# Split-operand matmuls that walk their columns from the last to the first

## What is computed

```python
for i in range(DEPTH):                      # DEPTH = 2
    h = rms_norm(x, attn_norm[i])
    proj = jnp.einsum('bsd,de->bse', h, w_in[i])          # 1024 x 3072
    sb = stick_breaking_attention(...)                    # 8 heads of 64
    df = differential_attention(...)                      # 4 heads of 2 x 64, values 128
    x = x + jnp.einsum('bse,ed->bsd', jnp.concatenate([sb, df], axis=-1), w_out[i])
    h2 = rms_norm(x, ffn_norm[i])
    if i % 2 == 0:
        x = x + swiglu(h2, dense_w_gate[j], dense_w_up[j], dense_w_down[j])    # width 2816
    else:
        x = x + moe_swiglu(h2, router_w[j], expert_w_gate[j], expert_w_up[j],
                           expert_w_down[j])              # top 2 of 8 experts, width 3584
return rms_norm(x, final_norm)
```

## Time and profile before

| | |
|---|---|
| median of the runs | 1404.23 us |
| span of the profiled execution | 1401.0 us |
| median less that span | 3.2 us |
| instructions in the trace | 19232 |

### The profile page before, as it was taken

The page is one execution under the profiler, slowest core; times in us unless marked ns, Lnnn a source line. Parts: engine busy times, 40 slices in busy tenths (PEclk is TensorE's granted clock), DMA queues, the critical chain, the costliest instruction groups (busy, mean ns, idle before and its releaser), DMA issues.

```text
span 1401.0 us, 19232 instructions
## 1 busy us (share of the span) xinstructions
PE 1386.3 (99%) x7369; PEld 1180.9 (84%) x7369; DVE 1139.5 (81%) x862; ACT 934.6 (67%) x751; POOL 37.4 (3%) x53
## 2 busy tenths in 40 slices
PE   9999999999999999999999999999999999999997
PEld 8888999889888888888888888888888888888885
DVE  6866565556857999888988888898888889889897
ACT  5555443445555877777777777777777777777775
POOL 0010000000010020000000000000000000001100
PEclk9999999999999999999999999999999999999999
DMA  9734985556424999999999999999999999999992
GB/s 336 265 114 147 393 326 187 191 170 199 155 98 163 356 389 393 396 394 397 371 395 390 361 387 392 374 371 389 394 350 396 391 361 383 393 378 364 396 395 114
DMA packets 191039, 448.80 MB, mean 320 GB/s; under 512 B 8515, under 2 KB 11274, under 8 KB 190986
## 3 DMA queue, kind: packets, MB, share of 16 engines
q1 hardware_dynamic: 189162, 441.74, 85.9%
q0 software_dynamic: 1616, 5.77, 1.0%
q10 hardware_dynamic: 208, 0.54, 0.1%
HBM read 429.67 MB, written 18.36 MB: 320 GB/s over the span
## 4 chain that ended last, share of the span: by engine, by line
PE 97%; DVE 1%; DMA 1%; ACT 1%; SPq 1%; issue 0%; DVEq 0%; ACTq 0%
PE ps L550 90%; PE ps L1009 2%; DMA raw<-in_w_in 1%; PE ps L681 1%; PE ps L712 0%; PE ps L968 0%; PE ps L735 0%; PE ps L670 0%; PE ps L639 0%; ACT w_hi L380 0%; PE ps L700 0%; PE ps L695 0%; PE ps L701 0%; PE ps L682 0%; PE ps L623 0%; PE ps L724 0%
## 5 line engine op out<-in xcount | busy, mean ns | idle before, releaser
L385 DVE TENSOR_TENSOR w_lo<-raw,w_hi 128x2048 fp32r<-128x2048 f32 x401 | 915.0, 2291 | 187.2 <-ACT w_hi L380 186.4
L380 ACT ACTIVATE w_hi<-raw 128x2048 fp32r<-128x2048 f32 x400 | 766.5, 1918 | 295.7 <-PE ps L550 286.7
L550 PE MATMUL ps<-w_hi,xe_hi 128*128 128x512 f32 x896 | 244.7, 395 | 0.6 <-DVE xe_lo L1846 0.6
L550 PE MATMUL ps<-w_hi,xe_lo 128*128 128x512 f32 x896 | 240.0, 390 | 0.0
L550 PE MATMUL ps<-w_lo,xe_hi 128*128 128x512 f32 x896 | 239.9, 389 | 0.0
L550 PEld LDWEIGHTS ps<-w_hi,xe_lo 128*128 128x128 f32 x896 | 168.2, 188 | 35.8
L550 PEld LDWEIGHTS ps<-w_lo,xe_hi 128*128 128x128 f32 x896 | 168.2, 188 | 35.4
L550 PEld LDWEIGHTS ps<-w_hi,xe_hi 128*128 128x128 f32 x896 | 164.6, 188 | 32.4 <-issue 0.8
L550 PE MATMUL ps<-w_hi,he_hi 128*128 128x512 f32 x448 | 120.9, 391 | 0.0
L550 PE MATMUL ps<-w_lo,he_hi 128*128 128x512 f32 x448 | 120.3, 390 | 0.0
L550 PE MATMUL ps<-w_hi,he_lo 128*128 128x512 f32 x448 | 120.1, 389 | 0.0
(11 more groups left out here) (250 smaller groups left out, 960.9 us busy)
## 6 DMA issues: line engine op xcount, KB each, us to landing
raw<-in_expert_w_gate SPq DMA_DIRECT2D x112, 1024.0 KB, 7.4
raw<-in_expert_w_up SPq DMA_DIRECT2D x112, 1024.0 KB, 7.5
raw<-in_expert_w_down SPq DMA_DIRECT2D x112, 1024.0 KB, 7.4
raw<-in_w_in SPq DMA_DIRECT2D x23, 1024.0 KB, 6.2
raw<-in_dense_w_gate SPq DMA_DIRECT2D x11, 1024.0 KB, 7.1
raw<-in_dense_w_up SPq DMA_DIRECT2D x11, 1024.0 KB, 7.6
raw<-in_dense_w_down SPq DMA_DIRECT2D x11, 1024.0 KB, 5.0
raw<-in_w_out SPq DMA_DIRECT2D x8, 1024.0 KB, 5.7
```

Source lines behind the costliest of these rows:

```text
L380: nc.scalar.activation(half_of(w_hi, n), raw[:, n % RAW, :], ACT.Copy).then_inc(hi_ready, 1)
L385: nc.vector.tensor_tensor(half_of(w_lo, n), raw[:, n % RAW, :], half_of(w_hi, n).bitcast(F32), ALU.subtract).then_inc(lo_ready, 1)
L550: return pe.matmul(o, stationary, moving, start=start, stop=stop, skip_group_check=True)
```

## The change

`add` now reverses the column axis of both the output and the moving operand. Column j of the product still lands at column j, but the engine takes the columns in falling order of address. The stationary operand and all other matmuls stay as they were. No instruction is added, removed or moved on any engine.

```diff
@@ -547,7 +547,7 @@
         def _(pe):
             def add(o, stationary, moving, start=False, stop=False):
 
-                return pe.matmul(o, stationary, moving, start=start, stop=stop, skip_group_check=True)
+                return pe.matmul(o[:, ::-1], stationary, moving[:, ::-1], start=start, stop=stop, skip_group_check=True)
 
             def keep_running(count, bank):
 
```

## The result

The changed kernel takes 1437.02 us (1436.02 to 1438.76, four runs) against 1404.56 us for the kernel before (1403.14 to 1405.26, four runs): a ratio of 1.0239, interval 1.0224 to 1.0253, or 32.5 us. The forecast was 1404 us in a range from 1340 to 1485, with 0.55 on no change.

A forecast was written before the change was run, and what follows sets the result against it. TensorE's matmuls were taken as the bound, L550 being 90% of the span. Terms 0 + 0 + 0 on the 1401.0 us span, plus 3.2 us up to the median of the runs, gave 1404 us, range 1340 to 1485.

The forecast's parts named there:

- Step (1), the reversed read: Reversed read and write in the 6504 matmuls of L550: no cost, 0.444 ns a column as now.
- The upper bound: Step (1) at the rate of L766's plain float32 products, 0.791 ns a column: L550 would take 990 us more.
- the gain: Case of a faster kernel, down to 1342 us; chance 0.15.
- the lost cycle: Rival with a slower kernel, 1479 us; chance 0.10, shared with smaller slowdowns at places not seen.
- The two arguments for zero: For step (1): backward jumps between matmuls are free, and the rate is the same for one bank or two in turn.
- f: Part of an L550 matmul's time that doesn't depend on its columns, from 113.4 and 227.1 ns: -0.3 ns, taken as nothing.
- Loss of pairing: Rival: falling moving reads or PSUM writes handle columns singly, not in pairs; 990 to 1270 us more, 2394 to 2674; chance 0.20.
- Steps (2) to (4): Between matmuls zero; VectorE and ScalarE as readers zero; any TensorE excess shows fully in the result.
- (2): Between matmuls: where turned follows unturned, order changes for one product only, delay at most 0.23 us; taken as zero.

The follow-up runs named there:

- e9: Kernel before plus 20 streams of 40 equal matmuls in front of the gather; 512 columns, 128 stationary: rising 227.5 ns, falling 233.5 ns per matmul.
- e13: Kernel before with moving and output columns in groups of 64, groups falling, rising inside: 1403.17 us against 1403.21, ratio 0.9999.
- e5: Kernel before with moving and output columns in groups of four (16 bytes), groups falling, rising inside: 1437.11 us.
- e7: Kernel before with moving and output columns in groups of sixteen (64 bytes), groups falling, rising inside: 1436.20 us.
- e2: Kernel before with only the output written in falling order, the moving operand read rising: 1403.25 us.
- e10: Kernel before with only the products that move 512 columns reversed, those of 256 columns left rising: 1435.50 us.
- e6: Kernel before with moving and output columns in groups of four (16 bytes), groups rising, falling inside: 1403.70 us.
- e12: Kernel before plus 19 streams of 40 matmuls, with shifted moving or stationary starts and groups of 64 falling; rising streams 9.09 to 9.46 us.
- e8: Changed kernel with the moved weight pieces placed 4 bytes further on in their slots: 1447.13 us.

## Why the prediction was wrong

- **Bound and path: right.** TensorE's column stream set the time, no new wait arose, the supply had slack, and the excess of the starts went straight into the result.
- **Step (1), the reversed read, is the step that failed.** I took its cost as nothing and forecast 1404 us. It is 6.3 ns for a product of 512 columns in the long stretches (27.4 us over all 4680) and up to 4.4 for one of 256 (6.2 us over all 1824). The upper bound held, but was too high by a factor of thirty (990 us against 33). That 1437 us lies within the range of 1340 to 1485 is luck. The two ends, the gain at 1342 us and the lost cycle at 1479, rest on a length of TensorE's clock cycle, and no run shows it. What the runs show in its place is the time of a column at 512 columns: 0.444 ns rising (227.1/512), 0.456 falling (233.4/512), 0.422 with bf16 in either direction (215.9/512, e9).
- **The two arguments for zero didn't bear on the question.** That the jump between products is free was read from f alone (next item). Falling groups of 256 bytes, with seven jumps backward in each 512-column product, do cost nothing (e13, 1403.17 us). That says nothing of the order within 256 bytes, where the price is (e5, e7). That the rate is the same for one PSUM bank and two was an argument on the write, which is free (e2, 1403.25 us).
- **f = -0.3 ns was a coincidence read as a law.** I took 113.4 and 227.1 ns as the nature of a product. The same chain had 117.8 ns for 144 rising products. A distance that comes in two sizes for one form asks for what makes it good, and thus for what could spoil it. The 0.444 ns a column that the pair gave was the falling price at 512 columns, 0.456 ns, less a discount.
- **The rivals.** Loss of pairing (0.20, 2394 us or more) is dead: even 16-byte pieces in falling order cost 3% (e5), not 80%. The lost cycle (0.10, 1479 us) was nearest in kind, a small additional price of a column, but it had 75 us where the two medians are 32.5 apart. The gain (0.15, down to 1342 us) isn't seen in any run: the lowest median of a kernel with turned reads is 1403.17 us (e13), beside 1403.21 for the kernel before, and no 4-byte stream of 512 columns had less than 226.7 ns.
- **Steps (2) to (4)** held in the time: zero between matmuls, zero for the readers, all of the excess on the path. But the reason in (2), that a change of order can touch one product only, doesn't hold in general: in e10 products that aren't turned are 4.4 ns slower through a stretch of over 900.

What stays open is what the discount is made of. Shown are conditions of it for 512 columns: 4-byte operands (bf16 has 215.9 ns in both directions), a moving read that rises across the pieces of a 256-byte run, a difference of a multiple of 256 bytes between the two operands' starts, stationary columns that are neighbours, and a size that follows their number. That it comes from a meeting of the two reads in the same memory would fit this, but is argued and not shown. For 256 columns even the conditions are open.

## What to carry to other kernels

Read the distance of starts of one form in every long stretch, not in one: two values for equal work mean that the fast one rests on a condition, here for 512 columns relative addresses, which an edit to order or layout can break without adding an instruction. Where products that move 512 float32-sized columns are streamed beside loads of 128 stationary columns, keep the moving read rising within each 256 bytes and its start a multiple of 256 bytes from the stationary one's; here that is worth 3% of their time (226.7 against 233.3 ns). The order of 256-byte groups, the order inside 16 bytes and the direction of the PSUM write cost nothing here (e13, e6, e2: 1403.17, 1403.70 and 1403.25 us).

## What the runs showed of the hardware that was not expected

- Rising 512-column products of 4-byte operands, streams of 40: 227.2 to 228.0 ns at offsets of 0 and 256 bytes, 229 to 233.5 at the multiples of 16 bytes tried between them, 236.5 at 4 bytes (e9, e12). Falling ones: 233.5 at every multiple of 16 bytes tried (but for one, 32 columns, at 236.5), 235.7 at 4 bytes (e8, e12).
- The discount shrinks with fewer stationary columns: a smaller load makes a rising stream slower, 227.5, 230.0, 231.8 ns for 128, 64, 32 columns (e9).
- In the whole kernels a rising stream of 256-column products keeps one of two distances, 113.3 or 117.8 ns, through hundreds of products, and a single float32 matmul of 256 columns between two stretches goes with a switch from one to the other (L874 and L754, in each of nine traces); a falling stream has 117.8 there.
- Falling writes to PSUM cost nothing (e2, 1403.25 us), nor do bf16 reads in falling order (e9, 215.9 ns either way).
